# Stick-breaking attention on one core: the low half of the transposed weights ahead of the scan in each VectorE slot

## The chip, the cores and the metric

The kernel runs on one core of a Trainium2 chip. The metric is device time in microseconds (us), the median of several executions. Below, TensorE is PE, VectorE is DVE, ScalarE is ACT, GpSimd is POOL, and SyncE, which issues the DMAs, is SP, as in the profile.

## The reference, cut to what matters

One layer for 2048 prompt frames and 32 sample frames: RMS norm, one projection to all heads' queries, keys, values and gates, two groups of attention heads, gates, an output projection and the residual. The change lies in the first group, stick-breaking attention, 8 heads of 64, strictly causal:

```python
def stick_breaking(q, k, v, q_pos, k_pos):
    z = jnp.einsum('bqhd,bkhd->bhqk', q, k).astype(jnp.float32) * (HEAD_DIM ** -0.5)
    mask = k_pos[None, :] < q_pos[:, None]
    log_keep = jnp.where(mask, jax.nn.log_sigmoid(-z), 0.0)
    after = lax.cumsum(log_keep, axis=3, reverse=True) - log_keep
    w = jnp.where(mask, jnp.exp(jax.nn.log_sigmoid(z) + after), 0.0)
    return jnp.einsum('bhqk,bkhd->bqhd', w.astype(v.dtype), v)
```

A weight is thus sigmoid(z) of its key times the product of sigmoid(-z) over all later keys that the query may see. The kernel forms that product with a running multiplication (a scan) along the keys, from the last to the first.

## The kernel before, in words

The program runs in stages: norm, two projection stages, the sample frames, the stick-breaking stage (`stick_breaking_stage`), and a tail. The stick-breaking stage is the longest; the rows below show its 320 slots from 978 us to 1730 us of the span. In it every engine has its own list of instructions, written out in the code, and semaphores tie the lists together. Each engine works its list strictly in order.

**Loops.** The frames are four blocks of 512 queries, q = 0 to 3. For each q there are four passes over a pair of heads, p = 0 to 3 (a hardware loop for p = 0 to 2, then the last pair written out). A pass has 2(q + 1) steps u: first head, then second, each over q + 1 blocks of 512 keys, from the diagonal block backwards. A step has four slots n = 0 to 3. For a step the slot number means a group of 128 queries (j) in the forward half and a group of 128 keys in the backward half. Slots are numbered through a pass below: slot 4u + n. The 80 steps make 320 slots.

**Forward half of a step** (the step two ahead of the current one, `nxt`): PE makes the scores (`front`, L1388 and L1389, into four PSUM banks c_score0 to 3, one for each j); ACT makes sigmoid(z) into c_take (L1264) and sigmoid(-z) in place in c_score (L1267); DVE scans c_score into c_kept (`scan`, L1328; on some steps a one-column copy, L1325, comes first); POOL multiplies c_take by c_kept into c_weight (L1220). A diagonal step has widths 128, 256, 384 and 512 instead of 512.

**Backward half** (the current step, `st`): PE transposes the weights (`turn`, L1400) into one of two PSUM banks c_turn0 and 1, in turn; ACT rounds the bank to the high half c_w_hi (`back_hi`, L1275); DVE subtracts it from the bank for the low half c_w_lo (`back_lo`, L1334); PE multiplies both halves by the values (`mix`, L1412 and L1414). `turn` of a slot waits for `back_lo` of two slots earlier, whose bank it reuses. At a head's end ACT and DVE add the two halves of the output (`finish`: ACT L1280, DVE L1339, called o_sum below); DVE's part waits for ACT's, which waits for the head's last `mix`.

**Output projection, mixed in.** For q > 0 each pass also projects 128 rows of the block before. ACT makes the gate's sigmoid in slot 0 (L957); DVE multiplies it by the gate (L961, `silu_gate`) and by the attention output (L967, `gate_o`); ACT rounds to p_m_hi (L973, `split_hi`); DVE makes the low half p_m_lo (L977, `split_lo`); PE then multiplies by the output weights in many slots (L990 to L992, `products`), first one half of the columns, then the other, into one PSUM bank. Between the two halves DVE must empty that bank by adding x (L1002, `residual`, p_y). The tables `SILU`, `GATE_O`, `SPLIT_LO`, `TILES` and `RESIDUAL` say in which slots: `gate_o` in slot 4 for q = 1, 5 otherwise; `split_lo` in slot 6 for q = 1, 7 otherwise; the first `residual` in slot 11, 16 and 18 for q = 1, 2 and 3, the second in slot 15, 23 and 30.

**DVE's slot before the change.** DVE does, in this order: the scan (in slot 0 the fourth of the following step, in slots 1 to 3 the first three of the step after that), `finish` of the head before where one is due, `back_lo`, and then what the tables put into the slot (`silu_gate`, `gate_o`, `split_lo`, `residual`). ACT's slot is: `finish` where due, `back_hi`, the two sigmoids, and its own share of the projection.

Of the kernel before, what the change touches and what calls it, by code (L numbers as in the profile page):

```python
# [36 lines left out]
def f32(ap):  # L37

    return ap.bitcast(F32)
# [965 lines left out]
def stick_breaking_stage(nc, s, proj):  # L1005
# [11 lines left out]
    with ExitStack() as ctx:  # L1017
# [53 lines left out]
        def step_after(q, p, u, last):  # L1071

            steps = 2 * (q + 1)
            if last and u >= steps:
                return Step(q + 1, 0, u - steps) if q < NSB - 1 else None
            return Step(q, p, u)

        def width(st, j):

            return P * (j + 1) if st.diagonal else SB  # L1080
# [22 lines left out]
        def residual_due(q, u, s):  # L1103

            return [half for half in range(2) if q and RESIDUAL[q][half] == 4 * u + s]

        def iterations(eng, body):


            for q in range(NSB):  # L1110
                with eng.Fori(0, PAIRS - 1) as p:
                    body(q, p, False)
                body(q, PAIRS - 1, True)
# [199 lines left out]
        @block.vector  # L1313
        def _(dve):
            def scan(st, j, initial=False):


                dve.wait_ge(keep_ready, 4 * st.number + j + 1)
                if not initial:
                    dve.wait_ge(weighted, 4 * st.number + j - 3)  # L1320
                    dve.wait_ge(scanned, 4 * st.number + j - 3)
                n = width(st, j)
                if st.slot and st.base:

                    dve.tensor_copy(kept[:, j, 2 * SB:2 * SB + 1], kept[:, j, 0:1])  # L1325
                above = 1.0 if st.diagonal else kept[:, j, 0:1] if st.base else kept[:, j, SB:SB + 1]
                out = kept[:, j, st.base:st.base + n]
                dve.tensor_tensor_scan(out[:, ::-1], score[j][:, n - 1::-1], one[:].to_broadcast([P, n]), above,  # L1328
                                       ALU.mult, ALU.bypass).then_inc(scanned, 1)

            def back_lo(st, n):
                dve.wait_ge(hi_ready, 4 * st.number + n + 1)
                c = slice(P * n if st.diagonal else 0, SB)
                dve.tensor_tensor(w_lo[n][:, c], turn_ps[n % 2][:, c], f32(w_hi[n][:, c]),  # L1334
                                  ALU.subtract).then_inc(lo_ready, 1)

            def finish(st):
                dve.wait_ge(o_lo_out, st.head + 1)
                dve.tensor_tensor(o_sum[st.e][0:HD, :], o_ps[0:HD, :], o_sum[st.e][HD:P, :],  # L1339
                                  ALU.add).then_inc(o_ready, 1)  # L1340

            def body(q, p, last):
                r = 4 * (q - 1) + p
                for u in range(2 * (q + 1)):
                    st, following, nxt = Step(q, p, u), step_after(q, p, u + 1, last), step_after(q, p, u + 2, last)
                    for n in range(QB):
                        if n == 0 and following:
                            scan(following, 3)
                        if n and nxt:
                            scan(nxt, n - 1)  # L1350
                        if n == 3 and u and Step(q, p, u - 1).last:
                            finish(Step(q, p, u - 1))
                        back_lo(st, n)
                        if q and 4 * u + n == SILU[q]:
                            proj.silu_gate(dve, r)
                        if q and 4 * u + n == GATE_O[q]:
                            proj.gate_o(dve, r)
                        if q and 4 * u + n == SPLIT_LO[q]:
                            proj.split_lo(dve, r)
                        for half in residual_due(q, u, n):  # L1360
                            proj.residual(dve, r, half)
                finish(st)

            dve.memset(one[:], 1.0)
            dve.memset(kept[:], 1.0).then_inc(start_done, 1)
            dve.wait_ge(start_done, 1)
            for j in range(QB):
                scan(Step(0, 0, 0), j, initial=True)
            for j in range(QB - 1):
                scan(Step(0, 0, 1), j)  # L1370
            iterations(dve, body)


# [482 lines left out]
```

## Time and profile before

| what | value |
|---|---|
| median of 3 runs | 1811.4 us (1809.9 to 1812.31) |
| the profiled execution | 1807.67 us, span 1805.7 us |
| instructions | 26062 |
| PE busy | 1522.5 us, 84% of the span |
| DVE busy | 1024.3 us, 57% |
| ACT busy | 874.6 us, 48% |
| POOL busy | 548.7 us, 30% |
| scans of 512 columns with a carried value (L1328) | 192, mean 1275 ns |
| low halves (L1334), all widths | 320, mean 592 ns |

The shares are means over the whole program; what a slot of the stick-breaking stage waits for is read from that stage alone. Instructions of one engine overlap a little at their ends, so the time that one takes of its engine is read from start to start. A number in square brackets with an arrow is idle time of the engine just before the instruction, and what ended it.

### The profile page before, as it was taken

To read this page: it belongs to the slowest core of one execution; us is meant where nothing else is said; L and a number is where in the kernel's file an instruction comes from. 1 tells how busy PE (TensorE), PEld (TensorE's weight loads), DVE (VectorE), ACT (ScalarE), POOL (GpSimd) and SP (SyncE) were. 2 spreads that over 40 slices of the span, in tenths; PEclk is the share of its full clock that TensorE was granted. 3 is DMA by queue.
4 is the path that set the end of the run, shared out by engine and by line. 5 is a ranking of instruction groups with operands and counts; after the bars stand their busy time and mean duration, and the time that the engine had idled before them with its cause. 6 is when DMAs were issued, how large, how long until landed. Compare 5 with 4: busy or idle time off the path is not lost. (4 is left out here: it accounts for less than half of the span.)

```text
span 1805.7 us, 26062 instructions
## 1 busy us (share of the span) xinstructions
PE 1522.5 (84%) x7514; PEld 1243.3 (69%) x7514; DVE 1024.3 (57%) x1469; ACT 874.6 (48%) x1864; POOL 548.7 (30%) x460
## 2 busy tenths in 40 slices
PE   4699969998999899999965667888789888878868
PEld 3577758886878687778754556666667666666657
DVE  5365615333443443354335767778888888888832
ACT  7322223433433353244323856557666677667621
POOL 1101011110101021012003855445454555555542
PEclk8799979998999899899986878889999999889989
DMA  5011133422432342234223543334432333333033
GB/s 190 27 50 54 52 120 116 133 68 77 137 102 65 113 138 65 78 105 129 83 87 106 194 123 119 115 102 136 134 110 73 111 114 105 100 109 99 4 98 115
DMA packets 181390, 183.07 MB, mean 101 GB/s; under 512 B 18448, under 2 KB 128904, under 8 KB 181304
## 3 DMA queue, kind: packets, MB, share of 16 engines
q1 hardware_dynamic: 181304, 181.92, 32.8%
q8 instruction: 55, 0.90, 0.2%
q14 instruction: 31, 0.25, 0.0%
HBM read 118.13 MB, written 63.93 MB: 101 GB/s over the span
## 5 line engine op out<-in xcount | busy, mean ns | idle before, releaser
L1220 POOL TENSOR_TENSOR c_weight<-c_take,c_kept 128x512 f32<-128x512 f32 (+2 forms) x320 | 346.0, 1099 | 321.1 <-PE c_turn L1400 201.4
L255 PE MATMUL b_ps<-XH,w_w_hi 128*128 128x512 f32 (+1 forms) x800 | 302.6, 378 | 14.4 <-issue 7.5
L256 PE MATMUL b_ps<-XL,w_w_hi 128*128 128x512 f32 (+1 forms) x800 | 300.7, 376 | 0.0
L257 PE MATMUL b_ps<-XH,w_w_lo 128*128 128x512 f32 (+1 forms) x800 | 299.2, 374 | 0.0
L1275 ACT ACTIVATE c_w_hi<-c_turn 128x512 fp32r<-128x512 f32 (+1 forms) x320 | 171.4, 536 | 185.1 <-PE c_turn L1400 184.0
L1400 PE MATMUL c_turn<-ident,c_weight 128*128 128x128 f32 x1088 | 192.3, 296 | 75.6 <-DVE c_w_lo L1334 72.1
L1328 DVE TENSOR_TENSOR_SCAN c_kept<-c_score,c_kept,c_one 128x512 f32<-128x512 f32 x192 | 244.9, 1275 | 18.4 <-ACT c_score L1267 17.0
L1334 DVE TENSOR_TENSOR c_w_lo<-c_turn,c_w_hi 128x512 fp32r<-128x512 f32 (+1 forms) x320 | 189.5, 592 | 78.4 <-ACT c_w_hi L1275 77.6
L1400 PEld LDWEIGHTS c_turn<-ident,c_weight 128*128 128x128 f32 x1088 | 142.0, 151 | 125.8 <-DVE c_w_lo L1334 83.5
L248 POOL TENSOR_TENSOR w_w_lo<-w_w_raw,w_w_hi 128x1024 fp32r<-128x1024 f32 x27 | 64.8, 2402 | 483.2 <-ACT w_w_hi L243 483.2
L666 ACT ACTIVATE b_raw<-b_ps 128x512 f32<-128x512 f32 x80 | 47.8, 598 | 304.3 <-PE b_ps L257 299.5
L255 PEld LDWEIGHTS b_ps<-XH,w_w_hi 128*128 128x128 f32 x800 | 155.5, 194 | 44.7 <-issue 16.8
L1264 ACT ACTIVATE c_take<-c_score 128x512 f32<-128x512 f32 (+2 forms) x320 | 171.3, 535 | 9.3 <-POOL c_weight L1220 3.6
L257 PEld LDWEIGHTS b_ps<-XH,w_w_lo 128*128 128x128 f32 x800 | 154.9, 194 | 29.2
L256 PEld LDWEIGHTS b_ps<-XL,w_w_hi 128*128 128x128 f32 x800 | 155.3, 194 | 27.1
L1267 ACT ACTIVATE c_score<-c_score 128x512 f32<-128x512 f32 (+2 forms) x320 | 173.0, 541 | 0.0
L1388 PE MATMUL c_score<-c_k,c_q_hi 128*128 128x512 f32 (+2 forms) x320 | 152.3, 476 | 11.4 <-POOL c_q_lo L1211 10.4
L715 DVE TENSOR_TENSOR b_pt_lo<-b_pt,b_pt_hi 128x512 fp32r<-128x512 f32 x64 | 44.2, 690 | 190.8 <-ACT b_pt_hi L647 190.6
L1412 PE MATMUL c_o<-c_w_hi,c_v 128*128 128x512 f32 (+1 forms) x320 | 128.1, 400 | 19.8 <-issue 11.6
L990 PE MATMUL p_ps<-p_w_hi,p_m_hi 128*128 128x512 f32 x192 | 87.5, 456 | 47.0 <-DVE p_y L1002 24.1
L1389 PE MATMUL c_score<-c_k,c_q_lo 128*128 128x512 f32 (+2 forms) x320 | 125.2, 391 | 0.0
L1414 PE MATMUL c_o<-c_w_lo,c_v 128*128 128x512 f32 (+1 forms) x320 | 124.8, 391 | 0.0
(231 smaller groups left out, 2790.2 us busy)
## 6 DMA issues: line engine op xcount, KB each, us to landing
c_k<-k_parts SPq DMA_DIRECT2D x80, 256.0 KB, 3.5
c_v<-v_parts SPq DMA_DIRECT2D x80, 256.0 KB, 3.5
w_w_raw<-in_w_in SPq DMA_DIRECT2D x27, 512.0 KB, 4.2
x_rows<-in_x_prompt SPq DMA_DIRECT2D x4, 2048.0 KB, 10.7
b_qraw<-normT SPq DMA_DIRECT2D x32, 256.0 KB, 4.1
k_parts<-b_kpart SPq DMA_DIRECT2D x16, 512.0 KB, 2.9
v_parts<-b_vpart SPq DMA_DIRECT2D x16, 512.0 KB, 3.1
gateT<-b_raw SPq DMA_DIRECT2D x32, 256.0 KB, 2.0
```

Source lines behind the costliest of these rows:

```text
L255: pe.matmul(out, w.hi[n][:, dt, :], xh, start=(dt == 0), stop=False)
L256: pe.matmul(out, w.hi[n][:, dt, :], xl, start=False, stop=False)
L257: last = pe.matmul(out, w.lo[n][:, dt, :], xh, start=False, stop=(dt == DT - 1))
L1220: pool.tensor_tensor(weight[:, st.par, j, 0:n], take[:, j, 0:n], kept[:, j, st.base + 1:st.base + n + 1], ALU.mult).then_inc(weighted, 1)
L1264: act.activation(take[:, j, 0:n], score[j][:, 0:n], ACT.Sigmoid, scale=SCALE)\
L1267: act.activation(score[j][:, 0:n], score[j][:, 0:n], ACT.Sigmoid, scale=-SCALE)\
L1275: act.activation(w_hi[n][:, c], turn_ps[n % 2][:, c], ACT.Copy).then_inc(hi_ready, 1)
L1328: dve.tensor_tensor_scan(out[:, ::-1], score[j][:, n - 1::-1], one[:].to_broadcast([P, n]), above, ALU.mult, ALU.bypass).then_inc(scanned, 1)
L1334: dve.tensor_tensor(w_lo[n][:, c], turn_ps[n % 2][:, c], f32(w_hi[n][:, c]), ALU.subtract).then_inc(lo_ready, 1)
L1388: pe.matmul(out, q_hi[st.e][:, P * j:P * j + P], keys, start=True, stop=False)
L1400: last = pe.transpose(turn_ps[n % 2][:, j * P:(j + 1) * P], weight[:, st.par, j, n * P:(n + 1) * P], s.ident[:])
L1412: pe.matmul(o_ps[:, c], v[st.e][:, st.slot, n, :], w_hi[n][:, c], start=(st.diagonal and n == 0), stop=False)
```

## The change

In each slot DVE now does `finish` where due, then `back_lo`, then the scan, and then what the tables put into the slot.

```diff
                     for n in range(QB):
+                        if n == 3 and u and Step(q, p, u - 1).last:
+                            finish(Step(q, p, u - 1))
+                        back_lo(st, n)
                         if n == 0 and following:
                             scan(following, 3)
                         if n and nxt:
                             scan(nxt, n - 1)
-                        if n == 3 and u and Step(q, p, u - 1).last:
-                            finish(Step(q, p, u - 1))
-                        back_lo(st, n)
                         if q and 4 * u + n == SILU[q]:
                             proj.silu_gate(dve, r)
```

No instruction is added or dropped, and only DVE's list changes. Three places show what that does to it. The names are those of the instructions above: c_kept is a scan, c_w_lo a low half, c_o_sum the head's end.

The first place is on DVE, in the last pass of q = 1, slots 10 to 12, around the first residual p_y. Before:

```order
L1334 TENSOR_TENSOR c_w_lo<-c_turn,c_w_hi 128x256
L1328 SCALAR_TENSOR_TENSOR c_kept<-c_score,c_one 128x384
L1339 TENSOR_TENSOR c_o_sum<-c_o,c_o_sum 64x512
L1334 TENSOR_TENSOR c_w_lo<-c_turn,c_w_hi 128x128
L1002 TENSOR_TENSOR p_y<-p_ps,p_x 128x512
L1328 SCALAR_TENSOR_TENSOR c_kept<-c_score,c_one 128x512
L1334 TENSOR_TENSOR c_w_lo<-c_turn,c_w_hi 128x512
```

Now:

```order
L1334 TENSOR_TENSOR c_w_lo<-c_turn,c_w_hi 128x256
L1328 SCALAR_TENSOR_TENSOR c_kept<-c_score,c_one 128x256
L1339 TENSOR_TENSOR c_o_sum<-c_o,c_o_sum 64x512
L1334 TENSOR_TENSOR c_w_lo<-c_turn,c_w_hi 128x128
L1328 SCALAR_TENSOR_TENSOR c_kept<-c_score,c_one 128x384
L1002 TENSOR_TENSOR p_y<-p_ps,p_x 128x512
L1334 TENSOR_TENSOR c_w_lo<-c_turn,c_w_hi 128x512
```

The 384-wide scan, which stood ahead of c_o_sum, now stands between the low half and p_y.

The second place is on DVE, in the last pass of q = 2, from its first slot to the gate's first product (slots 0 to 3). Before:

```order
L1328 SCALAR_TENSOR_TENSOR c_kept<-c_score,c_kept,c_one 128x512
L1334 TENSOR_TENSOR c_w_lo<-c_turn,c_w_hi 128x512
L1325 COPY c_kept<-c_kept 128x1
L1328 SCALAR_TENSOR_TENSOR c_kept<-c_score,c_kept,c_one 128x512
L1334 TENSOR_TENSOR c_w_lo<-c_turn,c_w_hi 128x384
```

Now:

```order
L1334 TENSOR_TENSOR c_w_lo<-c_turn,c_w_hi 128x512
L1328 SCALAR_TENSOR_TENSOR c_kept<-c_score,c_kept,c_one 128x512
L1334 TENSOR_TENSOR c_w_lo<-c_turn,c_w_hi 128x384
L1325 COPY c_kept<-c_kept 128x1
L1328 SCALAR_TENSOR_TENSOR c_kept<-c_score,c_kept,c_one 128x512
```

Ahead of the second low half (128x384) stood two scans of the pass; now one.

The third place is on DVE, at the end of the last pass of q = 2 (slots 22 and 23, and the head's end). Before:

```order
L1328 SCALAR_TENSOR_TENSOR c_kept<-c_score,c_kept,c_one 128x512
L1334 TENSOR_TENSOR c_w_lo<-c_turn,c_w_hi 128x512
L1002 TENSOR_TENSOR p_y<-p_ps,p_x 128x512
L1339 TENSOR_TENSOR c_o_sum<-c_o,c_o_sum 64x512
L1111 UNCONDITIONAL_BRANCH
```

Now:

```order
L1334 TENSOR_TENSOR c_w_lo<-c_turn,c_w_hi 128x512
L1328 SCALAR_TENSOR_TENSOR c_kept<-c_score,c_kept,c_one 128x512
L1002 TENSOR_TENSOR p_y<-p_ps,p_x 128x512
L1339 TENSOR_TENSOR c_o_sum<-c_o,c_o_sum 64x512
L1111 UNCONDITIONAL_BRANCH
```

The pass's last scan stood ahead of its last low half; now it stands between that low half and c_o_sum.

## Rows read from the trace of the kernel before

**Rows 1.** Stretches q = 0 to 3; busy us of PE, PEld, DVE, ACT, POOL; clock, DMA, GB/s.

```profile
985.00:1035.00 50.00, 34.76 (x194) 30.49 (x195) 35.89 (x59) 41.94 (x100) 43.53 (x41) 0.85 0.59 197
1035.00:1170.00 135.00, 103.46 (x489) 85.52 (x490) 93.57 (x120) 79.16 (x167) 68.86 (x57) 0.84 0.41 120
1170.00:1400.00 230.00, 190.85 (x962) 153.74 (x961) 182.68 (x244) 152.07 (x310) 114.14 (x104) 0.93 0.36 112
1400.00:1730.00 330.00, 274.50 (x1405) 219.74 (x1405) 280.21 (x371) 229.70 (x465) 173.97 (x154) 0.93 0.28 89
```

**Rows 2.** Waits of the stage, 975 to 1730 us: us in total, times, longest.

```profile
DVE c_w_lo L1334 <- ACT c_w_hi L1275: 77.6, 67, 7.4
...
DVE c_kept L1328 <- ACT c_score L1267: 36.6, 80, 3.9
...
PE p_ps L990 <- DVE p_y L1002: 24.1, 12, 2.6
PE p_ps L990 <- DVE p_m_lo L977: 22.8, 12, 2.5
```

**Rows 3.** Timeline of DVE, slots without a wait (start, length, instruction).

```profile
1575.37 0.66 DVE L1334 TENSOR_TENSOR c_w_lo<-c_turn,c_w_hi 128x512 fp32r<-128x512 f32 x1
1575.95 1.27 DVE L1328 TENSOR_TENSOR_SCAN c_kept<-c_score,c_kept,c_one 128x512 f32<-128x512 f32 x1
1577.14 0.66 DVE L1334 TENSOR_TENSOR c_w_lo<-c_turn,c_w_hi 128x512 fp32r<-128x512 f32 x1
```

**Rows 4.** Timeline around the first residual of a pass of q = 1.

```profile
1125.39 0.96 DVE L1328 TENSOR_TENSOR_SCAN c_kept<-c_score,c_one 128x384 f32<-128x384 f32 x1 [0.71 <-ACT c_score L1267]
...
1126.88 0.68 DVE L1339 TENSOR_TENSOR c_o_sum<-c_o,c_o_sum 64x512 f32<-64x512 f32 x1 [0.53 <-ACT c_o_sum L1280]
...
1127.80 0.68 DVE L1002 TENSOR_TENSOR p_y<-p_ps,p_x 128x512 f32<-128x512 f32 x1
...
1128.53 0.50 PE L990 MATMUL p_ps<-p_w_hi,p_m_hi 128*128 128x512 f32 x1 [1.76 <-DVE p_y L1002]
```

**Rows 5.** Timeline of a pass of q = 2, from the head's end to p_m_lo.

```profile
1342.79 0.68 DVE L1339 TENSOR_TENSOR c_o_sum<-c_o,c_o_sum 64x512 f32<-64x512 f32 x1 [0.86 <-ACT c_o_sum L1280]
...
1345.73 0.49 ACT L1275 ACTIVATE c_w_hi<-c_turn 128x384 fp32r<-128x384 f32 x1
...
1346.57 0.53 DVE L1334 TENSOR_TENSOR c_w_lo<-c_turn,c_w_hi 128x384 fp32r<-128x384 f32 x1
...
1354.28 1.21 DVE L967 TENSOR_TENSOR p_mixed<-p_mixed,p_o 128x1024 f32<-128x1024 f32 x1
...
1355.60 1.06 ACT L973 ACTIVATE p_m_hi<-p_mixed 128x1024 fp32r<-128x1024 f32 x1
...
1356.56 0.58 ACT L1275 ACTIVATE c_w_hi<-c_turn 128x512 fp32r<-128x512 f32 x1
...
1358.04 1.52 DVE L977 TENSOR_TENSOR p_m_lo<-p_mixed,p_m_hi 128x1024 fp32r<-128x1024 f32 x1
```

**Rows 6.** Timeline of q = 2 around the first residual of a pass.

```profile
1319.90 0.68 DVE L1339 TENSOR_TENSOR c_o_sum<-c_o,c_o_sum 64x512 f32<-64x512 f32 x1
...
1323.07 0.68 DVE L1002 TENSOR_TENSOR p_y<-p_ps,p_x 128x512 f32<-128x512 f32 x1
```

**Rows 7.** Timeline of q = 3, end of a pass and start of the next.

```profile
1589.13 0.60 ACT L1275 ACTIVATE c_w_hi<-c_turn 128x512 fp32r<-128x512 f32 x1
...
1591.49 0.66 DVE L1334 TENSOR_TENSOR c_w_lo<-c_turn,c_w_hi 128x512 fp32r<-128x512 f32 x1
...
1593.61 0.68 DVE L1339 TENSOR_TENSOR c_o_sum<-c_o,c_o_sum 64x512 f32<-64x512 f32 x1 [1.45 <-ACT c_o_sum L1280]
...
1596.03 0.49 ACT L1275 ACTIVATE c_w_hi<-c_turn 128x384 fp32r<-128x384 f32 x1
```

**Rows 8.** The instructions of L967: count, shortest, median and longest ns.

```profile
L967 DVE TENSOR_TENSOR p_mixed<-p_mixed,p_o x12: 1211/1406/1951, 1064.9 to 1675.9; 128x1024 f32<-128x1024 f32 x12
```

**Rows 9.** One stretch of q = 1 from p_m_lo's end on; columns as in rows 1.

```profile
1112.00:1119.00 7.00, 5.43 (x16) 4.53 (x17) 4.61 (x6) 1.72 (x5) 5.02 (x4) 0.55 0.32 78
```

## The prediction

> **What bounds the kernel now.** I read four views in this order: busy time by stretch, the waits of the stage, the timelines of DVE, ACT and PE around the places that the change touches, and the granted clock. In the table of stretches [rows 1] the reader is to see that q = 0 is close to POOL's own pace (43.5 of 50 us busy), and that from q = 1 on PE (70, 77, then 83 and 83%) and DVE (72, 69, 79, 85%) are about equally loaded, so neither mean names the bound. The waits of the stage [rows 2] show PE stopped twelve times for each of two results of DVE, p_m_lo and p_y, once per pass for q > 0. Those 46.9 us are on the path, since PE has nothing else in its list before those products. The timelines give the rest: from a head's end until p_m_lo, DVE runs almost back to back and the pass goes at DVE's pace; behind p_m_lo the projection's products fill PE, and the pass goes at PE's pace until its end. So a DVE delay counts if it lands on p_m_lo, on p_y or on the sum at the end of the pass, and mostly not elsewhere.
>
> **The change in the running slots.** Nothing is added. Where DVE has no waits, low half and scan alternate: 0.58 us from the start of a low half to the scan, 1.19 us from the scan to the next low half [rows 3]. Swapping them slides the row of scans back by one low half, and the slot still takes 1.77 us. Cost: 0 where DVE is back to back; where PE is the bound, covered by the product stream. What is left are the places where something of unequal length stands around the pair: pass starts, residuals and pass ends. SP's and POOL's lists are the same, and no DMA moves.
>
> **q = 0.** POOL's multiplications wait for a scan that now stands behind a low half of 0.58 us, but the high half that PE waits for comes no later. POOL's pace [rows 1] covers it: I take 0. Without that cover it is 0.58 in each of four passes, 2.3 us either way.
>
> **q = 1, first residual.** Before, the 384-wide scan stood ahead of the head's sum; now it stands between the low half and p_y. The sum waits 0.53 for ACT anyway [rows 4], so it does not come earlier, and p_y is later by the whole scan: 0.96 less the 0.08 by which scans overlap what follows (1.27 against 1.19, [rows 3]), 0.88. PE waits there 1.76 for p_y [rows 4], nothing hides it, and it becomes about 2.6. Four passes: **+3.5**. At the pass start the order costs about 0.06 each, +0.2.
>
> **q = 2, pass start.** Times from the head's sum at 1342.79 [rows 5]. Now: sum, low half 0 at 0.72, scan at 1.30, and DVE could take low half 1 at 2.49. But its high half comes from ACT at 1345.73 + 0.49 [rows 5], 3.43, and two scans no longer stand ahead of it. DVE idles 0.97, to 3.46. Ahead of gate_o (L967) stands the same set of instructions as before, so the delay is that idle time less a wait for c_score that no longer shows; such a wait is 36.6/80 = 0.46 us on average [rows 2]. Adding up the slots one by one I get gate_o at 12.02 instead of 11.49, +0.53. Behind it ACT's rounding, and the high half that ACT makes after that, follow in a fixed chain: gate_o lasts 1.21, p_m_hi starts 0.11 later, the next high half 0.96 after that and lasts 0.58 [rows 5], so it is there at 14.89. DVE in the meantime has only one low half and a short scan, and idles again, some 0.6. Then low half 7 (0.58), the 384 scan (0.88), and p_m_lo at 16.38, against 1358.04 - 1342.79 = 15.25 before. That is +1.13 in three passes; in the first pass of q = 2 only about 0.6 (the change's delay runs beside a transfer for gate_o, as I read that pass). Together **+4.0**. If ACT is quicker with its list when DVE is, the two idle times shrink; lower bound 0.
>
> **q = 2, first residual.** The sum of the head's end (1319.90) no longer has the scan ahead of it and comes up to 0.87 earlier, when ACT's part lets it; but a full scan now stands ahead of p_y. A scan costs 1.19, with its copy 1.25; 1.25 less 0.87 leaves nearly 0.4 on p_y (1323.07, [rows 6]); slot by slot, 0.35. Four passes: **+1.4**, between 0 and 1.25 x 4 = 5.
>
> **q = 3, pass start.** Same pattern, less severe: high half 1 is ready at 1596.03 + 0.49 - 1593.61 = 2.91 [rows 7], DVE is there at 2.49, idle 0.42 to 0.45. Four passes: **+1.8**, lower bound 0 if later waits absorb it.
>
> **q = 3, pass end.** Here the change gains. The last low half's high half is ready at 1589.13 + 0.60 = 1589.73, but that low half starts only at 1591.49 [rows 7], as it stands behind scans. With one scan fewer ahead it starts at about 1590.72, and last product, ACT's sum and DVE's sum follow: -0.77. The first residual of q = 3, 0.4 later by the same reckoning as for q = 2, is given back before that, since the scans' waits for c_score near the second residual vanish. Three passes at 0.77 and the last at about 0.66: **-3.0**. Upper end: 0, if the products keep PE busy until then.
>
> **A rule against the change.** gate_o, one of three 1024-wide instructions a pass, lasts 1.211 to 1.951 us, 1.406 in the middle [rows 8]; something collides with it at some places and not at others, and the change shifts these places. All twelve at the longest: (1.951 - 1.406) x 12 = +6.5; all at the shortest: -2.3. I take 0, as the count of neighbours stays.
>
> By the Trainium skill, "SBUF — State Buffer", section "Who interferes with whom", VectorE and GpSimd share a port pair under an exclusive lock, and a VectorE instruction with two SBUF inputs contends with a GpSimd instruction that reads SBUF, one blocking the other fully. The spread in [rows 8] agrees with it. By that rule each shift would go to one of the ends just named, and the sum with it.
>
> **Sum.** 3.5 + 0.2 + 4.0 + 1.4 + 1.8 - 3.0 = +7.9 us against the profiled execution, 1807.67, which gives 1815.6. That execution lies 3.7 below the median of the three runs, 1811.4; carried to the median the forecast is 1819.3.
>
> **Rivals.** A measurement of this kernel can tell about 0.2%, 3.6 us, from no change.
>
> *Forecast, slower by 7.9:* chance 0.40.
>
> *A, faster: the waits for c_score go.* DVE stops 80 times, 36.6 us, at a scan whose scores ACT has not made [rows 2], and the low half stands behind it. With the low half first it goes into that gap, and the bank for the next transpose comes free earlier. For it: those waits are certain to shrink. Against: most fall where PE is the bound and its products go on. To be faster by over 3.6, this must bring 3.6 + 7.9 = 11.5, about a third of it on the path. At half: -18.3 + 7.9 = -10.4, 1801. Chance 0.19.
>
> *B, no change: the pass starts are covered.* The idle times of q = 2 and q = 3 pass starts shift PE's projection, but PE gets its low halves earlier and catches up. Then 4.0 + 1.8 fall out: +2.1, 1813.5. Chance 0.20.
>
> *C, much slower: the clock.* In q = 1, behind a wait for p_m_lo, a stretch of 7 us ran at a mean clock of 0.55 [rows 9], so nearly all of it at 1.2 GHz. In q = 2 the stretches run at 0.93 on average [rows 1]. If PE's pause ahead of the products, 1.1 longer, sends it to the low level there also, up to 7 x 0.45 = 3.15 us a pass are lost: 4 x 3.15 = 12.6 on top, 1832. Against: it needs every pass of q = 2. Chance 0.17.
>
> By the Trainium skill, "TensorE: Matmul & The Clock Gate", section "Part 1: The HAM clock gate", the throttled half rate is the default state and activity releases it. [Rows 9] agree; by that rule a longer pause can only move toward C, which is why C has more than a small chance.
>
> *D, collisions all long:* +6.5 more, 1826. Chance 0.04. *That the change does not do what it says* is out: the order on DVE shows it at each place.
>
> **How the numbers follow.** Faster by over 3.6 is A, 0.19. No change is most of B and little else, 0.20. Slower is the forecast, C, D and the rest of B: 0.61. The range starts at 1803, which leaves out some 0.12 of A, and ends at 1831, which leaves out some 0.08 of C.
>
> **What would show it.** PE's waits for p_y [rows 2] go from 24.1 to about 30 (0.88 x 4 + 0.35 x 4 + 0.4 x 4 more), for p_m_lo from 22.8 to about 29, DVE's for c_score from 36.6 to under 10, and DVE's for c_w_hi from 77.6 to over 100. Passes of q = 1 grow by 0.9, of q = 2 by 1.5, of q = 3 shrink by up to 0.3. Wrong if p_y or p_m_lo wait no longer, or if the clock behind p_m_lo in q = 2 falls to the level of [rows 9].

## The result: slower by 0.9%, twice the forecast's distance

| | before | changed |
|---|---|---|
| median | 1811.66 us (1809.9 to 1812.31, 4 runs) | 1827.84 us (1826.86 to 1831.02, 4 runs) |
| ratio | | 1.0094, 95% interval 1.0076 to 1.0111 |
| profiled execution | 1807.67 us | 1827.67 us |

The direction and the range held (1819.3 was forecast, 1803 to 1831); the loss is 16.2 us between the medians where 7.9 was forecast. That the time lies inside the range is owed to the room left at its upper end for rival C, not to the sum. The two profiled executions differ by 20.0, since that of before lay some 4 us under its median. All that follows on places is read from these two.

**The stage as a whole.** The same times as in [rows 1], in the changed kernel, which has got a little less far in each:

```profile
985.00:1035.00 50.00, 35.65 (x187) 31.09 (x187) 33.31 (x55) 39.28 (x93) 42.32 (x40) 0.81 0.56 183
1035.00:1170.00 135.00, 98.89 (x479) 81.17 (x479) 90.47 (x118) 78.22 (x168) 68.15 (x57) 0.85 0.41 124
1170.00:1400.00 230.00, 186.75 (x917) 150.88 (x917) 170.87 (x235) 143.24 (x298) 112.99 (x99) 0.90 0.35 109
1400.00:1730.00 330.00, 268.94 (x1365) 215.63 (x1364) 275.60 (x364) 227.48 (x463) 181.32 (x154) 0.92 0.29 89
```

The granted clock (third number from the end) fell from 0.93 to 0.90 and from 0.93 to 0.92 in the two long stretches. The waits of the stage, against [rows 2]:

```profile
POOL c_weight L1220 <- DVE c_kept L1328: 228.9, 164, 6.4
...
DVE c_w_lo L1334 <- ACT c_w_hi L1275: 143.6, 144, 7.8
...
PE p_ps L990 <- DVE p_m_lo L977: 35.0, 12, 3.6
PE p_ps L990 <- DVE p_y L1002: 34.3, 12, 3.1
...
DVE c_kept L1328 <- ACT c_score L1267: 7.0, 6, 4.0
```

The waits for c_score are gone (36.6 to 7.0) and those for c_w_hi have doubled (77.6 to 143.6), as foreseen. PE's stops for p_m_lo and p_y (a stop is PE's idle time just ahead of the product that needs the result) have grown from 46.9 to 69.3 us together, by 22 where 12 were forecast. POOL, too, waits longer for scans (104.7 us before), but PE's weight loads stop for POOL's c_weight for only 3.2 us in the stage (13.2 before), so that is hidden.

**Pass by pass**, from the times of the heads' sums at the passes' ends (L1339), in us; the first pass of q = 0 counts from the span's start:

| | forecast | first pass | second | third | last | sum |
|---|---|---|---|---|---|---|
| q = 0 | 0 | -0.41 | +1.37 | +1.23 | -0.47 | +1.7 |
| q = 1 | +3.7 | +3.04 | -0.20 | -0.11 | +1.42 | +4.2 |
| q = 2 | +5.4 | +1.40 | +3.08 | +3.11 | +3.45 | +11.0 |
| q = 3 | -1.2 | 0.00 | -0.04 | +1.02 | +1.93 | +2.9 |

**The pass start of q = 2.** The timeline of the changed kernel's third pass of q = 2, the pass of [rows 5]:

```profile
1353.14 0.68 DVE L1339 TENSOR_TENSOR c_o_sum<-c_o,c_o_sum 64x512 f32<-64x512 f32 x1
...
1355.92 0.49 ACT L1275 ACTIVATE c_w_hi<-c_turn 128x384 fp32r<-128x384 f32 x1
1356.44 0.56 DVE L1334 TENSOR_TENSOR c_w_lo<-c_turn,c_w_hi 128x384 fp32r<-128x384 f32 x1 [0.70 <-ACT c_w_hi L1275]
...
1365.05 1.60 DVE L967 TENSOR_TENSOR p_mixed<-p_mixed,p_o 128x1024 f32<-128x1024 f32 x1
...
1366.76 1.06 ACT L973 ACTIVATE p_m_hi<-p_mixed 128x1024 fp32r<-128x1024 f32 x1 [1.61 <-DVE p_mixed L967]
...
1368.34 0.69 DVE L1334 TENSOR_TENSOR c_w_lo<-c_turn,c_w_hi 128x512 fp32r<-128x512 f32 x1 [0.49 <-ACT c_w_hi L1275]
...
1369.81 1.20 DVE L977 TENSOR_TENSOR p_m_lo<-p_mixed,p_m_hi 128x1024 fp32r<-128x1024 f32 x1
...
1371.15 0.49 PE L990 MATMUL p_ps<-p_w_hi,p_m_hi 128*128 128x512 f32 x1 [2.11 <-DVE p_m_lo L977]
```

Both idle times of DVE are there, 0.70 and 0.49 (0.97 and some 0.6 were forecast). From the sum, gate_o starts at 11.91 (forecast 12.02, before 11.49), and p_m_lo at 16.67 (forecast 16.38, before 15.25). It starts later than forecast, as gate_o now takes 1.60 instead of 1.21, but p_m_lo itself takes 1.20 instead of 1.52. Its end is later by 17.87 - 16.77 = 1.10. PE's stop grew from 0.92, which the first row below shows in before's third pass, to 2.11. That is the largest growth of the four passes: in the second pass before had 1.78 (second row), and the changed kernel has 2.14.

```profile
1359.69 0.49 PE L990 MATMUL p_ps<-p_w_hi,p_m_hi 128*128 128x512 f32 x1 [0.92 <-DVE p_m_lo L977]
...
1304.84 0.49 PE L990 MATMUL p_ps<-p_w_hi,p_m_hi 128*128 128x512 f32 x1 [1.78 <-DVE p_m_lo L977]
```

**The clock behind that stop.** The stretches from p_m_lo's end to p_y, and from p_y to the second p_y, of that third pass; first of before, then of the changed kernel (columns as in [rows 1], the clock third from the end):

```profile
1359.56:1377.94 18.38, 16.17 (x83) 12.96 (x83) 16.70 (x24) 13.12 (x27) 11.39 (x10) 1.00 0.26 69
1377.94:1396.12 18.18, 17.45 (x89) 14.84 (x89) 12.12 (x17) 10.70 (x21) 5.08 (x7) 0.91 0.12 41
```

```profile
1371.01:1391.35 20.34, 17.74 (x83) 14.19 (x83) 16.72 (x23) 12.73 (x26) 11.41 (x10) 0.92 0.23 71
1391.35:1410.41 19.06, 18.34 (x94) 15.66 (x95) 11.91 (x16) 10.81 (x22) 6.83 (x7) 0.91 0.07 26
```

The first stretch has the same 83 matmuls and is 1.96 us longer; PE is busy 1.57 us longer with them. Its clock is 0.92, not 1.00. A mean of 0.92 between the levels of 1.0 and 0.5 means 2 x 0.08 x 20.34, some 3.3 us at 1.2 GHz, in which half the work is lost: 1.6 to 1.7 us, as PE's busy time says. The remaining 0.4 fits the later p_y (next paragraph). Summed in this way, from the trace's own clock records, over p_m_lo to the pass's end in all twelve passes, before has 72 us at 1.2 GHz and the changed kernel 89. Half of the difference, 8.5 us, is a cost of the change that the sum didn't have.

**The residual of q = 2.** Timeline of the changed kernel, same pass:

```profile
1386.92 0.68 DVE L1339 TENSOR_TENSOR c_o_sum<-c_o,c_o_sum 64x512 f32<-64x512 f32 x1 [0.16 <-ACT c_o_sum L1280]
...
1390.16 1.27 DVE L1328 TENSOR_TENSOR_SCAN c_kept<-c_score,c_kept,c_one 128x512 f32<-128x512 f32 x1
1391.35 0.66 DVE L1002 TENSOR_TENSOR p_y<-p_ps,p_x 128x512 f32<-128x512 f32 x1
...
1392.07 0.74 PE L990 MATMUL p_ps<-p_w_hi,p_m_hi 128*128 128x512 f32 x1 [2.96 <-DVE p_y L1002]
```

From the sum to p_y it is 4.43 us; before it was 3.17 ([rows 6]): the scan of 1.25 that now stands between. The sum now waits for ACT (0.16), and PE's stop for it fell from 1.09 to 0.23. From p_m_lo's end to the sum it takes 15.91 us, before 15.20; less the 1.6 of the clock, the sum did come up by some 0.9.

**The pass end of q = 3.** Timeline of the changed kernel, end of the second pass, against [rows 7]:

```profile
1606.59 0.61 ACT L1275 ACTIVATE c_w_hi<-c_turn 128x512 fp32r<-128x512 f32 x1
...
1607.77 0.67 DVE L1002 TENSOR_TENSOR p_y<-p_ps,p_x 128x512 f32<-128x512 f32 x1
...
1608.35 0.68 DVE L1334 TENSOR_TENSOR c_w_lo<-c_turn,c_w_hi 128x512 fp32r<-128x512 f32 x1
...
1610.48 0.68 DVE L1339 TENSOR_TENSOR c_o_sum<-c_o,c_o_sum 64x512 f32<-64x512 f32 x1 [0.26 <-ACT c_o_sum L1280]
```

The last low half starts 1.15 behind its high half (1607.20), before 1.76: a gain of 0.61, where 0.77 was forecast.

### The profile page after: what moved, and what is told of

The parts are those of the page before. It is cut to its first block and busy times, and to the rows that moved or that the text cites. A ratio compares the mean times of both kernels' runs of the same rounds, so it can differ in the third digit from the quotient of the medians.

```text
span 1825.8 us, 26062 instructions
## 1 busy us (share of the span) xinstructions
PE 1529.6 (84%) x7514; PEld 1248.6 (68%) x7514; DVE 1017.2 (56%) x1469; ACT 872.0 (48%) x1864; POOL 560.7 (31%) x460
## 3 DMA queue, kind: packets, MB, share of 16 engines
q1 hardware_dynamic: 181304, 181.92, 32.4%
## 5 line engine op out<-in xcount | busy, mean ns | idle before, releaser
L1220 POOL TENSOR_TENSOR c_weight<-c_take,c_kept 128x512 f32<-128x512 f32 (+2 forms) x320 | 361.3, 1137 | 344.4 <-DVE c_kept L1328 228.9
L1334 DVE TENSOR_TENSOR c_w_lo<-c_turn,c_w_hi 128x512 fp32r<-128x512 f32 (+1 forms) x320 | 193.1, 604 | 145.6 <-ACT c_w_hi L1275 143.6
```

The costliest lines, as they stand in the source:

```text
L1220: pool.tensor_tensor(weight[:, st.par, j, 0:n], take[:, j, 0:n], kept[:, j, st.base + 1:st.base + n + 1], ALU.mult).then_inc(weighted, 1)
```

## The experiments

The theory: the change delays p_m_lo and p_y, and the longer stops that PE makes for them let its clock fall, which costs as much again. The rivals: pass starts alone; POOL; the order of the running slots itself. "Low" below is the time at 1.2 GHz from p_m_lo's end to the pass's end, summed over twelve passes as above, in the one profiled execution of each run: 72 us before, 89 with the change. In q = 1, which e2 leaves as it is in the changed kernel, it came to 36 us in e2 and 30 there, so differences of some 6 us between two runs may mean nothing. Each ratio is to the kernel before, measured together with the run: its median was 1812.52 beside e1 to e4, 1809.93 beside e5 to e8 and 1812.78 beside e9 to e12.

| run | median us | ratio (95% interval) | PE's stops for p_m_lo, p_y, us | low, us |
|---|---|---|---|---|
| e1, p_y ahead of the scan | 1810.06 | 0.9998 (0.9982 to 1.0015) | 32.4, 21.1 | 68 |
| e2, old order at pass starts | 1823.86 | 1.0051 (1.0022 to 1.0079) | 29.6, 34.4 | 89 |
| e3, matmuls added at p_m_lo | 1812.65 | 0.9998 (0.9976 to 1.0020) | 23.4, 34.3 | 55 |
| e4, before, matmuls added at p_y | 1800.69 | 0.9932 (0.9896 to 0.9969) | 23.0, 13.1 | 38 |
| e5, before, mix ahead | 1780.58 | 0.9830 (0.9768 to 0.9892) | 17.0, 14.4 | 30 |
| e6, before, p_m_lo twice in q = 2 | 1821.61 | 1.0056 (1.0031 to 1.0082) | 29.8, 24.2 | 82 |
| e7, p_y ahead, old start in q = 2 | 1804.05 | 0.9953 (0.9924 to 0.9982) | 30.7, 21.1 | 66 |
| e8, e7 and mix ahead | 1774.28 | 0.9795 (0.9735 to 0.9856) | 25.9, 11.3 | 31 |
| e9, e8, old order in more slots | 1767.61 | 0.9738 (0.9712 to 0.9764) | 23.6, 11.3 | 28 |
| e10, e9 and matmuls added | 1755.04 | 0.9675 (0.9652 to 0.9699) | 12.3, 11.3 | 0 |
| e11, the change and mix ahead | 1807.16 | 0.9975 (0.9954 to 0.9996) | 29.7, 24.6 | 50 |
| e12, before, mix ahead, matmuls added | 1770.57 | 0.9762 (0.9737 to 0.9786) | 6.9, 14.4 | 12 |

**e1, the residual ahead of the scan**, on the changed kernel:

```diff
                         back_lo(st, n)
+                        for half in residual_due(q, u, n):
+                            proj.residual(dve, r, half)
                         if n == 0 and following:
                             scan(following, 3)
...
-                        for half in residual_due(q, u, n):
-                            proj.residual(dve, r, half)
```

> The changed kernel with one thing undone: in the slots of a residual, DVE's p_y stands ahead of that slot's scan. Theory (a late p_y and p_m_lo, and TensorE's clock behind the longer pauses): p_y no longer has a scan of 0.88 (q = 1) or 1.25 us (q = 2 and 3) ahead of it, so 0.9 x 4 + 1.25 x 4 + 1.25 x 4 = 13.6 us come back, and up to 5 more where the stretch behind p_y fell to 1.2 GHz in the changed kernel and not before (q = 1 first and last pass, q = 3 third pass): 1809 to 1814. The rise of about 1.1 + 1.6 us a pass from the pass start to p_y in q = 2 stays. Rival (the loss comes from the pass starts alone): no more than 3 us come back, 1825 or more. Rival (POOL, whose waits for scans went from 104.7 to 228.9 us): the scan is no earlier, so nothing comes back.

Measured 1810.06, as the theory said. The waits of this kernel:

```profile
PE p_ps L990 <- DVE p_m_lo L977: 32.4, 12, 3.1
PE p_ps L990 <- DVE p_y L1002: 21.1, 12, 1.8
```

Only the stop for p_y shrank much (34.3 to 21.1, 13.2 us), and 17.8 us came back (20.6 between the profiled executions). Both rivals fall. Low time went from 89 to 68, of which half, some 10.5, would be the clock's part. With the 13.2 that makes 24, more than came back: not all of the shorter stops was gained, and how much each is worth this run doesn't tell.

**e2, the old order at the pass starts of q = 2 and 3**:

```diff
-                        back_lo(st, n)
+                        scan_first = q >= 2 and 4 * u + n <= SPLIT_LO[q]
+                        if not scan_first:
+                            back_lo(st, n)
...
+                        if scan_first:
+                            back_lo(st, n)
```

> The changed kernel with the old order, scan first, in the slots up to that of p_m_lo in the passes of q = 2 and 3, and the new order in all others. Theory: the passes of q = 2 get back 1.1 us up to p_m_lo, and those of q = 3 0.5: 0.6 + 3.3 + 2.0 = 6; and since PE's pause before p_m_lo is then 0.9 again, the 3.3 us at 1.2 GHz behind it go in three passes of q = 2 and perhaps the last of q = 3, 1.6 each: 5 to 6.5. Together 1815 to 1817. Without the clock (the stretch behind p_m_lo is longer by 1.6 for another reason): 1822, and the granted clock from p_m_lo to p_y in q = 2 stays at 0.92.

Measured 1823.86: the time missed the theory's 1815 to 1817 and lies near the 1822 of the expectation without the clock. The delay came back as expected: the stretch up to p_m_lo's end shrank by 1.25 to 1.36 in three passes of q = 2 and by 0.2 to 0.5 in q = 3, 5.7 us together. The clock's part did not come in sum. Two of the three passes of q = 2 lost their low stretch behind p_m_lo, but one of these got another behind p_y; the third kept it; and q = 3 got more from p_m_lo to p_y (18 to 22 us). Low time hardly moved. The second and the third pass of q = 2, from p_m_lo's end to p_y, and PE's stops ahead of these stretches:

```profile
1317.29:1336.08 18.79, 16.18 (x83) 12.96 (x83) 16.72 (x24) 12.73 (x27) 10.70 (x9) 1.00 0.26 82
1373.72:1394.01 20.29, 17.68 (x83) 14.14 (x83) 16.72 (x24) 12.74 (x27) 10.69 (x9) 0.92 0.25 72
```

```profile
1317.42 0.49 PE L990 MATMUL p_ps<-p_w_hi,p_m_hi 128*128 128x512 f32 x1 [1.78 <-DVE p_m_lo L977]
...
1373.86 0.79 PE L990 MATMUL p_ps<-p_w_hi,p_m_hi 128*128 128x512 f32 x1 [1.78 <-DVE p_m_lo L977]
```

One program, the same 83 matmuls and the same stop of 1.78: with the clock at 0.92 the stretch is 1.50 us longer than at 1.00, all of it PE's busy time. That is the price of a low stretch, with nothing changed in the program. It shows as well that the length of the last stop alone doesn't tell whether the clock falls.

**e3 and e4, matmuls added ahead of a stop**, four repeats of the slot's first score product, whose result is overwritten (the cuts are shortened); in e3 in the changed kernel ahead of p_m_lo, in e4 in the kernel before ahead of p_y (there with `(half, 0)` for half 1):

```diff
+                for _ in range(again):
+                    pe.matmul(score[j][:], q_hi[st.e][:, P * j:P * j + P], k[st.e][:, st.slot, :], start=True, stop=True)
                 pe.matmul(out, q_hi[st.e][:, P * j:P * j + P], keys, start=True, stop=False)
...
+                        tiles = projection_tiles(q, u, n)
+                        opens = any((half, 0) in tiles for half in (0,))
                         if nxt:
-                            front(nxt, n)
+                            front(nxt, n, again=4 if opens else 0)
```

> The changed kernel with four matmuls of 512 columns more (a repeat of the first score product of the slot, overwritten) in the slot in which PE stops for p_m_lo, ahead of that stop, so that PE's pause there is about 0.94 us shorter at the same p_m_lo. If the pause sets the clock: the low clock from p_m_lo to p_y in q = 2 goes (granted clock 0.92 to 1.00), and each of the three passes gains 1.6 us although PE has more to do: about -5, and up to -2 in q = 3. If the clock follows something else: no gain, and the added matmuls cost 0 (they lie in the pause) to 12 x 0.94 = 11 us where the pause is shorter than they are.

> The kernel before, with the same four added matmuls in the slot in which PE stops for p_y, whose pause is about 1.7 us. If pauses of this size set the clock: behind p_y the kernel before ran some 3.3 us at 1.2 GHz in most passes (granted clock 0.91 to 0.93 from the first p_y to the second in q = 2 and 3); with a pause of about 0.8 it stays at 2.4 GHz in these, 1.6 us gained in each of 9 to 11 passes: 14 to 18 us less, 1793 to 1798. If not: 1811 to 1816.

Measured 1812.65 and 1800.69: with more work, 15.2 us faster than the changed kernel and 11.8 faster than the kernel before. The stretches of the third pass of q = 2, e3 from p_m_lo to p_y and e4 from p_y to the second:

```profile
1366.51:1385.28 18.77, 16.17 (x83) 12.96 (x83) 16.72 (x24) 12.69 (x26) 11.41 (x10) 1.00 0.26 74
```

```profile
1373.48:1390.08 16.60, 15.87 (x89) 13.49 (x89) 12.20 (x16) 11.03 (x23) 5.07 (x7) 1.00 0.12 43
```

In e3 the clock is 1.00 instead of 0.92 and the stretch 18.77 instead of 20.34; in e4 it is 1.00 and 16.60 instead of 18.18. In both, p_m_lo and p_y are no earlier: what was taken away is idle time of PE ahead of the product (its stops for p_m_lo went from 35.0 to 23.4 us in e3, though in the pass shown only from 2.11 to 1.75) and with it the low clock. In e3, some 35 us of low time less, half of it 17, agree with the 15.2. That is twice what was expected, since low time fell in q = 1 and q = 3 as well, from 62 to 38 us. e4 gained less than the 14 to 18 expected: low time fell by some 35 us, worth 17, and the passes behind the first of q = 0 are 15.1 us shorter in its profile, but that first pass ended 4.5 us later, for which no cause was sought.

**e5, mix ahead**, on the kernel before:

```diff
-                        for half, tile in projection_tiles(q, u, n):
-                            proj.products(pe, 4 * (q - 1) + p, half, [tile])
+                        tiles = projection_tiles(q, u, n)
+                        opens = any((half, 0) in tiles for half in (0, 1))
+                        if not opens:
+                            for half, tile in tiles:
+                                proj.products(pe, 4 * (q - 1) + p, half, [tile])
                         if n < 3 and u:
                             mix(Step(q, p, u - 1), n + 1)
-                        if n == 3 and not late:
+                        if n == 3:
                             mix(st, 0)
-                        if late:
-                            mix(st, 0)
+                        if opens:
+                            for half, tile in tiles:
+                                proj.products(pe, 4 * (q - 1) + p, half, [tile])
```

> The kernel before, but in the two slots of a pass in which PE stops for p_m_lo and for p_y, the slot's mix (two matmuls, 0.46 us) is issued ahead of the product that stops instead of behind it: 0.46 us of work that has to be done anyway goes into each of 24 pauses. Theory (pauses set the clock): 24 x 0.46 = 11 us from the work alone, and more where a pause becomes short enough for the clock to stay at 2.4 GHz; the added matmuls of 0.94 us kept it there behind p_y, half of that may do it in some passes: 1788 to 1802. Rival (only the length of the work counts, not the clock): 1801, and the time at 1.2 GHz from the first p_y to the second stays at 3.3 us in q = 2.

Measured 1780.58, better than expected: 29 us, of which 11 are the work put into the stops, and 42 us of low time less give 21; the two make 32, against 31.3 between the profiled executions.

**e6, the cost by itself**: the kernel before with p_m_lo made twice in q = 2, no order changed.

```diff
+        if first is not None:
+            dve.tensor_tensor(self.m_lo[:, :, 0:cols], self.mixed[:, :, 0:cols], f32(self.m_hi[:, :, 0:cols]),
+                              ALU.subtract).then_inc(first, 1)
+            dve.wait_ge(first, nth)
```

> The kernel before, with p_m_lo made twice in the passes of q = 2 alone, so that PE's pause ahead of it grows from 0.92 to about 2.4 us and nothing else moves: the suspected cost by itself, without the change of order. Theory: 1.45 us for the late product in each of four passes (less in the first), and 3.3 us at 1.2 GHz behind it in the three passes of q = 2 that have none there, 1.6 each: q = 2 passes longer by 2.6 to 3.1, together 9 to 12 us, about 1822. Rival (the extra 1.6 us from p_m_lo to p_y in q = 2 comes from the new order of scans and low halves, not from the pause): 1.45 x 4 = 5.8, about 1818, and the clock from p_m_lo to p_y stays at 1.00.

Measured 1821.61, as the theory said. The passes of q = 2 are longer by 0.90, 2.82, 2.84 and 2.85 us. The third one from p_m_lo to p_y:

```profile
1372.18:1392.13 19.95, 17.75 (x83) 14.17 (x83) 16.80 (x23) 12.74 (x26) 11.37 (x10) 0.91 0.18 48
```

The same 83 matmuls as before, PE busy 1.58 us longer with them, the clock at 0.91 and the stretch 1.57 longer (18.38 before). PE's stop ahead of it is 3.04 (0.92 before; some 2.4 was expected). So a later p_m_lo brings the extra 1.6 us behind it without the new order. With the change the stretch is 0.39 longer still (20.34), which fits the scan that stands ahead of p_y there.

**e7 to e12, what the order is worth without its losses.** e7 joins e1 with e2's condition for q = 2 alone; e8 adds e5's edit; e9 puts `q == 0 or q >= 2` into the condition in place of `q == 2`; e10 adds e3's matmuls ahead of p_m_lo; e11 is the changed kernel with e5's edit alone, e12 the kernel before with e5's edit and those matmuls.

> The changed kernel with both suspected losses undone: p_y ahead of the scan in the slots of a residual, and scan first in the slots of q = 2 up to that of p_m_lo. What is left of the change is the order low half, scan in all other slots. Theory: on top of the run with p_y ahead (1810), p_m_lo of q = 2 comes 1.1 us earlier in three passes and 0.5 in one, and its pause is 0.9 as before, so the clock behind it stays high more often: 4 to 8 us less, 1802 to 1806, below the kernel before. Rival (the pass start cost nothing by itself): 1809 to 1811.

> The same with the slot's mix ahead of the product that stops for p_m_lo or p_y, as in the run with the kernel before. Theory: the gains add up, 0.46 x 24 = 11 us and some clock: 1785 to 1797, below the kernel before and below both of the others. Rival (both remedies shorten the same pauses, so they don't add): no better than the better of the two.

> The best kernel so far (1774.3), with scan first also in all slots of q = 0 and in the slots of q = 3 up to that of p_m_lo, so that low half first is left only where DVE runs without a pass start or a residual beside it. Theory: the passes of q = 0 get back their 1.4, 1.2 and -0.5 us, and those of q = 3 0.5 each up to p_m_lo: 2 + 2 = 4 us less, 1768 to 1772, if the clock does not answer otherwise. Rival (what is left of low half first is worth nothing): then it is no better than the kernel before with mix ahead, 1780.

> The same with the four added matmuls in the slot in which PE stops for p_m_lo. In q = 1 and 3 the stretch from p_m_lo to p_y still has 3.3 to 6 us at 1.2 GHz in about seven passes: theory, 1.6 us or more come back in each of those, 11 us, less what the added matmuls overrun the pause by in q = 2 (0.94 us of work against a pause of about 0.45: 0.5 x 4 = 2): 1758 to 1766. Rival (the low clock there comes from the slots ahead, in which PE waits for DVE, and not from the last pause): no gain and the overrun, 1771 to 1776.

> The changed kernel with nothing undone, and the slot's mix ahead of the product that stops. Theory (the change costs a late p_m_lo and p_y, some 8 us, and the clock behind the longer pauses, another 8 to 12): with mix in the pause part of the clock comes back, but the pauses stay longer than in the kernel before with mix ahead (1780.6), by 1.1 and 0.9 to 1.25 us: between that plus 8 and plus 20, 1789 to 1801. Rival (the loss is not in those pauses): 1827.8 - 24 x 0.46 = 1817 or just below.

> The kernel before with mix ahead (1780.6) and the four added matmuls ahead of the stop for p_m_lo: the same remedies without any part of the change. Theory: in that run the stretch from p_m_lo to p_y had 3.5 to 6 us at 1.2 GHz in six passes of q = 1 and 3; about 1.6 us comes back in each, less 2 us of overrun: 1771 to 1777. Against the run with the rest of the change, it tells what low half first is worth in the running slots: theory, 5 to 12 us, from the low clock and the ends of the passes of q = 3; rival, nothing.

Measured 1804.05, 1774.28, 1767.61, 1755.04, 1807.16 and 1770.57. e7 fell where the theory put it, e9, e10 and e12 up to 3 us under it, e8 some 11 under it (low time 66 in e7 and 31 in e8: the clock gave more than was allowed for); e11 missed. The 2 us that e10 and e12 allowed for added matmuls overrunning the stops of q = 2 were not needed: those stops were some 1.3 us in e9, and 0.4 is left of them in e10. In e11 PE's stops stay at 54.3 us against 31.4 in e5, and low time at 50 against 30: half of 20 is the clock's, which leaves 14 of the 24 us between the two profiled executions (1800.43 and 1776.35) for the delays; the medians are 26.6 apart. With the change in place, the stops for p_y in q = 2 and 3 are still 2.5 us or more in e11, against 1.3 to 2.1 in e5: a remedy of 0.46 us is too short for them. The fastest, e10, has the clock at 1.00 from p_m_lo on in every pass; its q = 3, second pass, p_m_lo to p_y, where before had 0.89 and 23.40 us:

```profile
1503.58:1523.38 19.80, 19.13 (x104) 15.71 (x104) 16.80 (x24) 14.62 (x30) 9.27 (x9) 1.00 0.20 53
```

e10 beats both kernels, by 3.25% and by 4%. It does 48 matmuls whose result is thrown away. Against e12, which has the same remedies and no part of the change, it is 15.5 us faster, where 5 to 12 were expected: the low half first, with p_y ahead of the scan and the old order at the pass starts, is worth that much, once the stops are short. Some 6 of it are the clock (low time 12 in e12, none in e10).

**All stops together.** The fourteen profiles, of both kernels and e1 to e12, have 336 stops of PE for p_m_lo or p_y. The table sorts them by length and counts those with over 0.3 us at 1.2 GHz behind them, up to the next p_y:

| PE's stop | number | with low clock behind |
|---|---|---|
| under 1.6 us | 113 | 6 |
| 1.6 to 2.0 us | 76 | 46 |
| 2.0 us and more | 147 | 126 |

Longer stops go with the low clock, in all kernels together. Between 1.6 and 2.0 us it went either way, as in e2; what decides there stays open.

## Why the prediction was right in direction and half in size

- **Running slots, 0.** Nothing in the changed kernel showed against it, and the rivals on POOL and on the order itself fell (e1, e6). That the order is worth something once the stops are short, e10 against e12 shows.
- **q = 2, pass start, +4.0.** Measured 1.09 to 1.18 up to the end of p_m_lo in each pass, 4.5 together; in the first pass, too, where 0.6 was expected. The mechanism is right, by the two idle times that were named; that the number fits so well is partly luck. The idle times are shorter (1.19 together, 1.57 forecast), gate_o takes 0.39 longer and p_m_lo 0.32 less.
- **q = 2, first residual, +0.35 a pass.** The stretch grew by about 2.0 in three passes; less 1.6 for the clock, 0.35 to 0.5. Right.
- **q = 3, pass start, +0.45 a pass.** Measured 0.34, 0.54, 0.52 and 0.52 up to p_m_lo's end. The mechanism is right (DVE idles 0.35 for high half 1 at the pass start of [rows 7]); gate_o takes 0.6 longer there and p_m_lo 0.54 less, which cancel by luck.
- **q = 1, first residual, +0.88 a pass.** p_y does come 0.86 later behind the head's sum in all four, as forecast. But only the first and last pass show a loss (+3.04, +1.42), with a new low stretch behind p_y in each; in the others the scan's delay was given back before. Between the previous pass's end and p_m_lo's end they gained 0.3 to 0.5: gate_o takes 1.20 instead of 1.95 there, a collision gone. Low time fell there by 1.0 to 1.4 us between p_m_lo and p_y as well.
- **q = 3, pass end, -3.0.** From p_m_lo to the end of the pass the four measured -0.34, -0.60, +0.50 and +1.41, +1.0 in all: the gain is there where the clock let it be (0.61 on the last low half), not in the last pass, and lost in the third to a new low stretch of 3.4 us. Low time grew by 3.7 us over the four; less half of that, the gain is some 0.8, not 3.0.
- **q = 0, 0.** Measured +1.7, inside its bounds of 2.3. e9, with the old order there, got the second pass back to 15.01 us (before 14.92, changed 16.29); the third stayed long. What of it is clock and what delay stays open.
- **gate_o, 0.** The twelve went from a sum of 18.26 to 18.77 us, but the twelve p_m_lo, which the text did not price, from 18.42 to 14.39: 4 us gained, spread over the passes. What collides is POOL, as rows of the changed kernel's third pass of q = 2 show:

```profile
1364.30 1.27 POOL L1220 TENSOR_TENSOR c_weight<-c_take,c_kept 128x512 f32<-128x512 f32 x1 [0.98 <-DVE c_kept L1328]
...
1369.97 1.76 POOL L1220 TENSOR_TENSOR c_weight<-c_take,c_kept 128x384 f32<-128x384 f32 x1 [1.32 <-DVE c_kept L1328]
```

POOL's first multiplication ends at 1365.57, behind the start of gate_o (1365.05), and gate_o ends at 1366.65, 1.08 later. At p_m_lo's start (1369.81) POOL is idle: it takes 1.20, and POOL's next multiplication, which starts into it, is the one held up (1.76, for 0.87 in before's pass). Over the fourteen profiles gate_o and p_m_lo take 1.19 to 1.23 us in the 160 cases in which no POOL instruction is running at their start (or one that ends within 0.03 us), and end 1.08 to 1.09 us behind the end of the running one in the other 180. So what counts is what POOL is doing when they start, not how many neighbours they have, which the prediction took as unchanged.

**The step that failed is the sum's silence on the clock.** It took each delay at its own length, with PE's work behind it as long as before. With the longer stops the low clock cost 8.5 us more in the profiled executions; of the 20.0 between these, 7.9 were forecast, and the other 3.6 lie mostly in q = 0 (1.7) and in the pass ends of q = 3 (some 2.2 short of their -3.0). Between the medians the clock's part is smaller. The profiled execution of before had a granted clock of 0.913 over the whole program, the median of its 53 executions beside e1 to e12 0.910, the changed kernel 0.908: that is some 10 us of low time more, or 5 us (an estimate from three-digit means) of the 8.3 by which 16.2 passes the forecast. Rival C named this mechanism for q = 2 and priced it too high per pass (3.15, measured 1.5 to 1.6) and in too few places: it came in three passes of q = 2 behind p_m_lo, but also behind p_y in the first and last pass of q = 1 and in the third of q = 3. It was given 0.17, on the ground that it "needs every pass of q = 2"; it should have been a term of the sum, since [rows 9] and the 0.91 behind p_y in q = 2 already showed such stretches behind stops. Its price came from [rows 9], which do not begin at p_m_lo's end, as their heading says, but 0.16 ahead of its start, so that they hold part of PE's stop as well:

```profile
1112.16 1.36 DVE L977 TENSOR_TENSOR p_m_lo<-p_mixed,p_m_hi 128x1024 fp32r<-128x1024 f32 x1
```

By the Trainium skill, "TensorE: Matmul & The Clock Gate", section "A second HAM failure mode: psum-queue depth-cycling", one kernel's TensorE paused briefly and often between groups of matmuls, and its clock swung between the two levels. These runs agree: behind 126 of 147 stops of 2 us or more the low level came.

Rival A's waits for c_score did vanish, and no gain came of it in the changed kernel. The reason given against it, that PE was the bound there, fits that, but no run tests it by itself. With the stops short (e10 against e12) a gain does show.

## What to carry to other kernels

Price a delay on a busy TensorE twice: once by its length, once by what the clock does behind the stop, and read the second from the stretches behind stops that the trace already has. Where a stop can't be removed, issue ready work ahead of it: two matmuls moved by a line gave more than the whole order of another engine's list took or gave. When a reordering loses, find the one or two places of unequal work beside the swapped pair before dropping it; undone there, the rest was a gain (e7, 0.5% under the kernel before). And when one DVE instruction shows several lengths, look at what POOL is running when it starts.

## What the runs showed that was not expected

Matmuls whose result is thrown away made the program faster, by 15.2 us in e3, where 5 to 7 were expected, and by 11.8 us in e4. One further stretch at 1.2 GHz behind a stop of 2 to 3 us costs 1.5 to 1.6 us in a stream that is full, more than the delay of 1.1 that lengthened the stop. gate_o and p_m_lo, held up by a running POOL instruction, end 1.08 to 1.09 us behind it, in all 180 cases. And executions of one kernel differ by more than was assumed: 1806 to 1828 in 53 of the kernel before. The clock goes with the time there: over the whole program the four fastest had 0.914 or 0.915 granted, the four slowest 0.902 to 0.904. e10, which has no low stretch behind p_m_lo, stayed within 1753.45 to 1756.18, but in four executions only, and the changed kernel's four lie nearly as close (1826.86 to 1831.02); that fewer low stretches narrow the spread is not shown.
